# Moving the latent branch's queries, index scores and attention units to later slots in a two-layer encoder kernel

## The reference

```
score = jnp.einsum('bqh,bhqs->bqs', wib, jax.nn.relu(dots))      # C's indexer
_, idx = lax.top_k(score, topk)                                   # 64 of up to 256 keys
...
merged = (gates[:, :, 0] * (ya @ a_w_out) + gates[:, :, 1] * (yb @ b_w_out)
          + gates[:, :, 2] * (yc @ c_w_out) + gates[:, :, 3] * (yd @ d_w_out))
x = x + merged @ w_o
```

## Time and profile before

| | us |
|---|---|
| median of 3 runs | 822.85 (822.40 to 823.03) |
| profiled execution | 822.7 |
| its span, first to last instruction | 821.0 |
| TensorE busy | 804.7 |
| VectorE busy | 560.2 |
| ScalarE busy | 404.1 |
| TensorE's idle before act_lo (L1005) | 6.5 |
| TensorE's idle before x's load | 4.9 |
| TensorE's idle before w_lo (L988) | 1.7 |

### The profile page before, as it was taken

The page is one execution under the profiler, slowest core; times in us unless marked ns, Lnnn a source line. Parts: engine busy times, 40 slices in busy tenths (PEclk is TensorE's granted clock), DMA queues, the critical chain, the costliest instruction groups (busy, mean ns, idle before and its releaser), DMA issues.

```text
span 821.0 us, 10180 instructions
## 1 busy us (share of the span) xinstructions
PE 804.7 (98%) x3860; PEld 657.5 (80%) x3860; DVE 560.2 (68%) x841; ACT 404.1 (49%) x553; POOL 45.1 (5%) x84
## 2 busy tenths in 40 slices
PE   4999999999999999999999999999999999999998
PEld 3888777778888888888888877777788888888886
DVE  8789687894675664456568987798685764565443
ACT  5757455453364444344356656556342644444430
POOL 6240000000000000000004100000000000000000
PEclk8999999999999999999999999999999999999999
DMA  7735446465375655565664545364545564665541
GB/s 204 284 102 182 139 163 211 134 201 202 96 246 175 205 180 179 169 208 190 176 209 136 172 153 180 113 220 157 201 156 192 166 206 155 206 203 185 174 154 51
DMA packets 99681, 144.38 MB, mean 176 GB/s; under 512 B 12081, under 2 KB 63025, under 8 KB 99633
## 3 DMA queue, kind: packets, MB, share of 16 engines
q1 hardware_dynamic: 99632, 143.73, 54.0%
HBM read 142.54 MB, written 1.05 MB: 175 GB/s over the span
## 4 chain that ended last, share of the span: by engine, by line
PE 90%; DVE 5%; SPq 2%; DMA 1%; POOL 1%; issue 1%; ACT 1%; DVEq 0%; ACTq 0%
PE big L1432 18%; PE big L1436 18%; PE big L1435 18%; PE mix L1436 10%; PE mix L1432 10%; PE mix L1435 10%; DVE w_lo L988 2%; SPq L552 1%; PE mix L1765 1%; PE mix L1458 1%; DMA w_raw<-in_w_in 1%; PE mix L1547 1%; POOL rstd L626 1%; PE mix L1502 1%; PE mix L1535 1%
## 5 line engine op out<-in xcount | busy, mean ns | idle before, releaser
L647 ACT ACTIVATE w_hi<-w_raw 128x2048 fp32r<-128x2048 f32 (+2 forms) x140 | 256.6, 1837 | 160.6 <-DMA w_raw<-in_w_gate_up 88.1
L988 DVE TENSOR_TENSOR w_lo<-w_raw,w_hi 128x2048 fp32r<-128x2048 f32 (+3 forms) x139 | 301.1, 2181 | 44.0 <-ACT w_hi L647 43.5
L1432 PE MATMUL big<-w_hi,act_hi 128*128 128x512 f32 (+2 forms) x480 | 188.7, 393 | 8.2 <-DVE act_lo L1005 6.5
L1435 PE MATMUL big<-w_lo,act_hi 128*128 128x512 f32 (+2 forms) x480 | 183.9, 383 | 0.0
L1436 PE MATMUL big<-w_hi,act_lo 128*128 128x512 f32 (+2 forms) x480 | 183.7, 383 | 0.0
L1432 PE MATMUL mix<-w_hi,act_hi 128*128 128x512 f32 x352 | 137.4, 390 | 0.0
L1436 PE MATMUL mix<-w_hi,act_lo 128*128 128x512 f32 x352 | 137.1, 390 | 0.0
L1435 PE MATMUL mix<-w_lo,act_hi 128*128 128x512 f32 x352 | 137.0, 389 | 0.0
L1432 PEld LDWEIGHTS big<-w_hi,act_hi 128*128 128x128 f32 x480 | 90.8, 189 | 30.0 <-DVE act_lo L1005 7.2
L1436 PEld LDWEIGHTS big<-w_hi,act_lo 128*128 128x128 f32 x480 | 90.8, 189 | 17.5
L1435 PEld LDWEIGHTS big<-w_lo,act_hi 128*128 128x128 f32 x480 | 91.0, 190 | 15.5
(11 more groups left out here) (190 smaller groups left out, 696.1 us busy)
## 6 DMA issues: line engine op xcount, KB each, us to landing
w_raw<-in_w_in SPq DMA_DIRECT2D x44, 1024.0 KB, 5.1
w_raw<-in_w_gate_up SPq DMA_DIRECT2D x88, 512.0 KB, 4.8
w_raw<-in_w_down SPq DMA_DIRECT2D x22, 1024.0 KB, 4.9
w_raw<-in_w_o SPq DMA_DIRECT2D x8, 1024.0 KB, 5.1
w_raw<-in_b_w_out SPq DMA_DIRECT2D x4, 1024.0 KB, 5.4
w_raw<-in_w_in SPq DMA_DIRECT2D x4, 904.0 KB, 6.1
w_raw<-in_w_in SPq DMA_DIRECT2D x4, 512.0 KB, 3.6
w_raw<-in_a_w_out SPq DMA_DIRECT2D x4, 512.0 KB, 4.0
```

The lines of the kernel that those rows point to most:

```text
L647: nc.scalar.activation(high(u), arrived(u), ACT.Copy).then_inc(hi_ready.sem, 1)
L988: nc.vector.tensor_tensor(low(u)[:, a:], arrived(u)[:, a:], high(u)[:, a:].bitcast(F32), ALU.subtract).then_inc(lo_by_dve, 1)
L1432: ins = nc.tensor.matmul(dst[:, 0:w], xh, wh, start=first and n == 0, stop=False)
L1435: nc.tensor.matmul(dst[:, 0:w], xh, wl, start=False, stop=False)
```

## The change

- B's keys keep their place in slots 5 and 6 (two heads). C's four queries are normed and rotated in VectorE's steps of slot 12, behind C's key and behind a wait for TQ's second half; they go to `roped_a`, which B's queries used. Their signal is a new one, `J`.
- TK turns two pairs (one bank) in slot 8; the other two pairs become TJ in slot 16.
- TensorE's index products move from slots 7 and 9 to 10 and 14; VectorE's `index_scores` from 7 and 9 to 12 and 15 (`INDEXED_AT`), ScalarE's copies with the products.
- In the bank list the products of block 1 (banks 0 and 1) now stand between S of unit 0 and S of unit 1.
- The attention units 4 and 5 (C's) take all their steps two slots later: S in 23 and 25, T in 25 and 27, Y in 26 and 28.
- The selection rounds are spread anew: slots 12, 15, 16, 17 have 3, 1, 2, 2 rounds of block 0 (before: 12 and 16 with 5 and 3), slots 18, 20, 21, 22, 23 have 2, 2, 1, 2, 1 of block 1 (before: 18, 20, 21, 22 with 1, 3, 2, 2).

```diff
@@ -140,11 +140,13 @@
-PE_AT = {"wT": 3, "latT": 4, "TI": 5, "kv": 6, "idx0": 7, "TK": 8, "idx1": 9, "TQ": 11, "TC": 15,
+PE_AT = {"wT": 3, "latT": 4, "TI": 5, "kv": 6, "TK": 8, "idx0": 10, "TQ": 11, "idx1": 14, "TC": 15, "TJ": 16,
          "spatial": 12, "mixed": 12, "yaT": 13, "ydT": 14}
-S_AT = [13 + 2 * i for i in range(len(ATTN))]
-T_AT = [15 + 2 * i for i in range(len(ATTN))]
-Y_AT = [16 + 2 * i for i in range(len(ATTN))]
+
+S_AT = [13, 15, 17, 19, 23, 25]
+T_AT = [15, 17, 19, 21, 25, 27]
+Y_AT = [16, 18, 20, 22, 26, 28]
+INDEXED_AT = (12, 15)
 def mixer_uses():
@@ -153,15 +155,18 @@
     uses = turned("hT")
     uses += [(("wT",), 0), (("latT",), 1), (("TI", 0), 2), (("TI", 1), 3), (("kv",), 0),
-             (("idx", 0, 0), 0), (("idx", 0, 1), 1), (("TK", 0), 2), (("TK", 1), 3), (("idx", 1, 0), 0), (("idx", 1, 1), 1),
+             (("TK", 0), 2), (("idx", 0, 0), 0), (("idx", 0, 1), 1),
              (("TQ", 0), 2), (("TQ", 1), 3), (("spatial",), 1), (("mixed",), 2),
-             (("yaT",), 3), (("S", 0, 0), 0), (("S", 0, 1), 1), (("ydT", 0), 2), (("ydT", 1), 3), (("TC",), 3)]
+             (("yaT",), 3), (("S", 0, 0), 0), (("S", 0, 1), 1), (("idx", 1, 0), 0), (("idx", 1, 1), 1),
+             (("ydT", 0), 2), (("ydT", 1), 3), (("TC",), 3)]
     for i, (m, _, tb) in enumerate(ATTN):
         if i + 1 < len(ATTN):
             for k in range(2):
                 uses.append((("S", i + 1, k), k))
         for k in range(turned_blocks(i)):
             uses.append((("T", i, k), 2 + k))
+        if i == 0:
+            uses.append((("TJ", 0), 2))
         uses.append((("Y", i), 3 if m == "B" else 2))
     uses += turned("mT") + turned("h2T")
@@ -199,8 +204,9 @@
 DVE_ANGLES = 3 + len(TURNS) + 2 + len(TWO_PI) + 2
 DVE_CONSTS = DVE_ANGLES + 2 + 2 * len(D_POOLS)
-TOPK_AT = {12: (0, 0, 5), 16: (0, 5, 8), 18: (1, 0, 1), 20: (1, 1, 4), 21: (1, 4, 6), 22: (1, 6, 8)}
-DVE_STEPS = 123
+TOPK_AT = {12: (0, 0, 3), 15: (0, 3, 4), 16: (0, 4, 6), 17: (0, 6, 8), 18: (1, 0, 2), 20: (1, 2, 4), 21: (1, 4, 5),
+           22: (1, 5, 7), 23: (1, 7, 8)}
+DVE_STEPS = 132
 class Signal:
@@ -336,7 +342,7 @@
         act_lo_ready = signal_from_1("act_lo_ready", 8)
         lat_normed = signal("lat_normed", 1)
         wt_masked = signal("wt_masked", 1)
-        roped = {n: signal(f"roped_{n}", 1) for n in "IKQC"}
+        roped = {n: signal(f"roped_{n}", 1) for n in "IKQCJ"}
         za_squared = signal("za_squared", 2)
         gelu_arg = signal("gelu_arg", 2)
         gelu_tanh = signal("gelu_tanh", 2)
@@ -806,7 +812,9 @@
                             drain(l, logits[:, odd::2, 0:keys(tb)], "idx", tb, odd,
                                   src=score_view(mix_bank("idx", tb, odd), tb), func=ACT.Relu, scale=SCALE * 0.5)
                 if s == PE_AT["TK"]:
-                    drain_pairs(l, "TK", 7, 2)
+                    drain_pairs(l, "TK", 7, 1)
+                if s == PE_AT["TJ"]:
+                    drain_pairs(l, "TJ", 9, 1)
                 for tb in range(TB):
                     if s == 9 + tb:
                         act.wait_ge(*gelu_arg.nth(l, tb + 1))
@@ -1044,9 +1052,9 @@
             def norm_heads(l, name, tile, tb, gains):
-                heads = tile.shape[2]
-                v = tile[:, tb]
-                step(l, nc.vector.tensor_tensor(v, v, norm_factor(l, name)[:, 0:heads].unsqueeze(2)
+                first, heads = gains[0][0], gains[-1][1] - gains[0][0]
+                v = tile[:, tb, first:first + heads]
+                step(l, nc.vector.tensor_tensor(v, v, norm_factor(l, name)[:, first:first + heads].unsqueeze(2)
                                                 .to_broadcast([P, heads, HD]), ALU.mult))
                 for h0, h1, g in gains:
                     last = nc.vector.tensor_tensor(tile[:, tb, h0:h1], tile[:, tb, h0:h1],
@@ -1267,8 +1275,8 @@
                     if s == 4 + tb:
                         head_squares(l, f"K{tb}", 6)
                     if s == 5 + tb:
-                        norm_heads(l, f"K{tb}", heads_b, tb, [(0, 2, 1), (2, 6, 2)])
-                        rope(l, "K", heads_b, roped_b, tb, 6, [(0, 2, 2, 0), (2, 6, 1, 4)], tb == 1)
+                        norm_heads(l, f"K{tb}", heads_b, tb, [(0, 2, 1)])
+                        rope(l, "K", heads_b, roped_b, tb, 2, [(0, 2, 2, 0)], tb == 1)
                     if s == 6 + tb:
                         head_squares(l, f"Q{tb}", 8)
                     if s == (7, 9)[tb]:
@@ -1285,9 +1293,12 @@
                     step(l, ins)
                     for tb in range(TB):
                         rope(l, "C", heads_c, roped_c, tb, 1, [(0, 1, 2, 0)], tb == 1)
+
+                    dve.wait_ge(*mix_is_full(l, "TQ", 1))
+                    for tb in range(TB):
+                        norm_heads(l, f"K{tb}", heads_b, tb, [(2, 6, 2)])
+                        rope(l, "J", heads_b[:, :, 2:6], roped_a, tb, 4, [(0, 4, 1, 0)], tb == 1)
                 for tb in range(TB):
-                    if s == PE_AT[f"idx{tb}"]:
-                        index_scores(l, tb)
                     if s == 8 + tb:
                         gelu_args(l, tb)
                     if s == 10 + tb - (1 if tb else 0):
@@ -1298,6 +1309,9 @@
                     v_norm(l)
                 if s == PE_AT["spatial"]:
                     gated(l)
+                for tb in range(TB):
+                    if s == INDEXED_AT[tb]:
+                        index_scores(l, tb)
                 if s == PE_AT["yaT"]:
                     y_low(l, 1, y_ac_hi[:], y_ac_lo[:], 0.5, "yaT")
                 if s == PE_AT["ydT"]:
@@ -1580,7 +1594,10 @@
                         scores(l, ("idx", tb), tb, 0, 2)
                 if s == PE_AT["TK"]:
                     pe.wait_ge(*roped["K"].nth(l, 1))
-                    turn_pairs(l, "TK", 7, roped_b, 4)
+                    turn_pairs(l, "TK", 7, roped_b, 2)
+                if s == PE_AT["TJ"]:
+                    pe.wait_ge(*roped["J"].nth(l, 1))
+                    turn_pairs(l, "TJ", 9, roped_a, 2)
                 if s == PE_AT["TQ"]:
                     pe.wait_ge(*roped["Q"].nth(l, 1))
                     turn_pairs(l, "TQ", 3, roped_a, 4)
```

## The result

The changed kernel takes 829.39 us (median of four runs, 828.44 to 830.47) where the kernel before takes 822.94 in the same comparison: ratio 1.008, interval 1.0068 to 1.0091. It is slower, as forecast, but by 6.5 us instead of 2.0, and outside the range. Run again later it took 826.74 us (five runs, 826.59 to 828.29; ratio 1.0052, 1.0038 to 1.0066), which lies inside the range; experiments 10 and 11 take up the difference. The profiled execution took 829.98 us, 828.2 of span. A few executions took over 1000 us (one each of experiments 5 and 7, two of the kernel before); ranges and ratios leave them out, the medians count them (at most 0.2 us lower without), and as the one of experiment 5 is the one that was traced, that experiment is read by its times alone.

What follows compares the result with a forecast made beforehand. TensorE, busy 98% of the span, was taken as the bound, so only its waits could be gained. With a new bank wait at slot 14, 822.7+0.66 (layer 0)+1.45 (layer 1) = 824.8 us, range 821.0 to 827.0.

Steps and rivals of the forecast that it cites:

- The old wait and its price: Slot 10: TensorE's wait for unit 11's low weights goes in both layers, -1.30 and -0.97 us.
- The landing and VectorE's chain: Unit 13 lands at 72.04 us, VectorE enters slot 12 at 79.1, unit 0's row maximum is there at 96.2.
- TensorE's arrival: Layer 0: slot 13's last matmul comes at 95.40 us; TensorE then waits 2.1 us for the S0 banks at slot 14.
- Behind slot 14: Later work stays covered: no second wait at unit 17, unit 23 or T3, costed at nothing.
- the three uncertain margins: Unit 17's split 0.7 us in hand, unit 23's 1.4, T3's row 0.5; if short, up to 1 us each.
- TJ costs its 0.43 us: Slot 16: the other half of the turns, moved there from slot 8, adds 0.43 us.
- The attention units' move: S4/S5 units moved by two slots, taken as free: as many groups, as many slots that hold one.
- Layer 0 to slot 17: Layer 0 is 0.23 us behind at slot 14's ydT, plus 0.43 for TJ in slot 16: +0.66 us.
- the term of the late load: Layer 1, unit 12's load: +1.03 us if on time, +2.85 if as late as before; +1.45 taken.
- halfway: Layer 1: lateness of unit 12's load taken halfway, delaying the chain 0.4 us, for +1.45 us.
- my sum: Whole kernel: 822.7+0.66+1.45 = 824.8 us.
- The clock: Rival: the new slot 14 wait drops TensorE's clock, costing 2 to 3 us a layer, 830 us; chance 3%.

Runs made afterwards that it cites:

- 10: The changed kernel run again unaltered: 826.74 us (five runs), ratio 1.0052 against the kernel before.
- 11: The changed kernel run a third time unaltered, for a second trace of it: 826.77 us for the single look.
- experiment 5: Changed kernel with the latent queries put back in slots 5 and 6, turned in slot 8, no TJ: 820.81 us, ratio 0.9976.
- 7: As experiment 5 (index scores' move alone), with the first three selection rounds in slot 13: 820.48 us, ratio 0.9968.
- experiment 1: Changed kernel with slot 12's three selection rounds moved to slot 13, behind unit 0's row maximum: 820.47 us, ratio 0.9973.
- experiment 4: Kernel before with only the latent queries' norm, rotation and turn moved (slot 12 and TJ): 823.89 us, ratio 1.0013.
- 12: As experiment 4, with VectorE alone combining block 1's index scores in slot 10 rather than 9: 823.32 us, ratio 1.0007.
- experiment 3: Changed kernel with nine unread products on TensorE ahead of block 1's index scores in slot 14: 825.26 us, ratio 1.0035.
- 8: As experiment 3, with four unread products instead of nine: 826.91 us, ratio 1.0045.
- experiment 6: Changed kernel with the ydT mixing products ahead of block 1's index scores on TensorE in slot 14: 826.28 us, ratio 1.0038.
- 9: Changed kernel with one selection round more in slot 12, moved ahead from slot 15: 830.08 us, ratio 1.0089.
- 2: Changed kernel with one of slot 12's three selection rounds put into slot 13: 823.38 us, ratio 1.0007.

## Why the prediction was right in its mechanism and wrong in its size

**The old wait and its price: right.** No wait on w_lo is left, and experiment 1 gains 2.3 us where 1.30+0.97 were counted, although it pays the 0.35 us of the attention units (below) out of it. That the 4.04 us of index scores suffice for it is shown by the times of experiment 5 and the trace of 7; that the queries' part alone does not end it, by experiment 4.

**The landing and VectorE's chain: right.** ScalarE took up unit 13 at 72.00 us (72.04 forecast), VectorE came to slot 12 at 79.14 (79.1) and the row maximum ended at 96.15 (96.2). From VectorE's timeline of the changed kernel:

```profile
79.14 0.47 DVE L1290 SCALAR_TENSOR_TENSOR heads_c<-heads_c,rstd,g_head 128x64 f32<-128x64 f32 x2
...
95.98 0.17 DVE L1159 TENSOR_SCALAR row<-row 128x4 f32<-128x4 f32 x1
```

**TensorE's arrival: right within 0.3 us.** The last matmul of slot 13 started at 95.13 instead of 95.40, so the wait was 2.4 us of pitch (2.69 less the usual 0.32) instead of 2.1.

**Behind slot 14: right.** No wait stands at unit 17, unit 23 or T3; the three uncertain margins held, at nothing. (In experiments 4 and 12 the margin of unit 17 did not hold, for about 0.25 us.) TJ costs its 0.43 us (between slots 15 and 17 the distance to the kernel before grows from 1.74 to 2.17 us).

**The attention units' move: a small term put at nothing.** I took it as free, "as many groups, as many slots that hold one". The count was wrong: from slot 21 on TensorE's small groups stand in six places before (144.85, 151.54, 157.84, 164.96, 171.16 and 177.62 us) and in seven after (146.94, 152.96, 159.25, 171.06, 178.21, 184.36 and 190.80). From slot 17 to behind these groups the distance grows from 2.17 to 2.35 us in layer 0 and from 7.07 to 7.24 in layer 1, about what entering and leaving one more group cost by my own count, 0.2 us. It grows by 0.18 us in layer 0 of experiments 1 and 7 as well, which move these units, and not at all in that of 4 and 12, which don't. No run took the move back alone.

**Layer 0 to slot 17: right but for the clock.** The first matmul of slot 17 in the two layers, of the changed kernel and then of the kernel before:

```profile
121.98 0.48 PE L1446 MATMUL big<-w_hi,act_hi 128*128 128x512 f32 x1
...
527.74 0.48 PE L1446 MATMUL big<-w_hi,act_hi 128*128 128x512 f32 x1
```

```profile
119.81 0.48 PE L1432 MATMUL big<-w_hi,act_hi 128*128 128x512 f32 x1
...
520.67 0.48 PE L1432 MATMUL big<-w_hi,act_hi 128*128 128x512 f32 x1
```

Layer 0 is 2.17 us behind there. Less 1.56 for the clock that is 0.61, where +0.66 was forecast; experiments 3 and 8, whose clock stayed at full, are 0.70 us behind at the same place.

**Layer 1: the term of the late load, too small.** The distance grows from 2.17 to 7.07 us; 0.28 of that comes in before layer 1's slot 6 (454.60 against 452.15 us at its first matmul), 0.18 of it by the attention units' move, and 0.1 has no cause that I found. Of the other 4.62, the clock is 2.59 and 2.03 are left, where I took 1.45, between 1.03 with the load on time and 2.85. The load of unit 12 was late again:

```profile
473.14 1.92 ACT L653 ACTIVATE w_hi<-w_raw 128x2048 fp32r<-128x2048 f32 x1 [2.15 <-DMA w_raw<-in_w_in]
...
476.52 0.69 DVE L1120 SCALAR_TENSOR_TENSOR probs_t<-merged,probs_t 128x512 f32<-128x512 f32 x1 [3.49 <-ACT merged L821]
```

ScalarE stood 1.2 to 2.25 us for it in all ten traces that could be read of a version with the index scores moved, much as in the one of before, so that "halfway" had no ground. The price of the late load varies with it. Counted the same way, layer 1 cost 2.03, 1.80 and 1.65 us in the three traces of the changed kernel, 1.29 in experiment 3 (ScalarE stood 1.23 us) and 3.20 in experiment 8 (2.25 us). The forecast of 1.45 lies among them, its span of 1.03 to 2.85 almost covers them (the 1.03 is itself 0.07 more than its terms, 0.66 and 0.3, give). The cause of the late load was not tried. Without the clock, the profiled execution would have taken 829.98-4.15 = 825.8 us: my sum, this 0.6, and 0.4 of which nearly all is the attention units' move. Experiment 3, in which the clock never falls in slot 14, took 825.26.

**The clock: the step that failed.** The sum took the wait of 2.1 us at its length alone, with nothing for the clock behind it. I wrote that a 1.03 us wait left it at full, one of more than 2 us at the start did not (that one was 6.0 us long by the timeline), and that "waits of 2 to 4 us lie between", and gave the fall 3%. The forecast itself put waits of 2.1 us and more, twice, into that unknown stretch. Nothing in the trace of before spoke for 3%; the price that I gave (2 to 3 us a layer, 830 us) was a little high (1.56 and 2.59 us were measured), and the case should have had a large share of the chances and the upper end of the range. In the three traces it fell in one layer or both, at 1.5 to 4.15 us in all; the mean clocks of the other executions speak for the same. The Trainium skill ("TensorE: Matmul & The Clock Gate", "HAM oscillation"), which I named beside it, says that waits of TensorE drop the clock and each drop is paid again: the traces agree, with 1.56 and 2.59 us in the two layers of one execution. The page speaks of longer gaps than most of these; here the measurement decides.

## What to carry to other kernels

When work is moved off a late engine, follow the engine that becomes early to its next shared buffer and look in which order that buffer is granted: here TensorE came 3 us earlier to banks that are free only behind VectorE's row maximum, and moving three selection rounds behind the row maximum, the change of one number, turned 829.4 us (or 826.7) into 820.5. A new wait of some 2 us on a TensorE that has none is to be priced with a fall of the clock behind it, and filled with other products if it cannot be removed. Moving work off an engine gains only if the next thing in its order isn't pinned to someone else, as the queries' move alone shows.

## What the runs showed of the hardware that I had not expected

How long TensorE stood idle in one wait does not by itself tell whether the granted clock falls. Idle time ahead of block 1's scores in slot 14, and the clock behind it, in the ten traces where that time could be read (experiment 3's has no record of the clock; its matmuls keep their length):

| run | layer 0: idle us, clock | layer 1: idle us, clock |
|---|---|---|
| changed kernel | 2.30, fell | 3.21, fell |
| changed kernel again (10) | 2.48, fell | 2.99, full |
| changed kernel again (11) | 2.12, fell | 2.82, full |
| four rounds (9) | 3.08, full | 3.68, fell |
| four products (8) | 1.39, full | 2.77, full |
| mixing products first (6) | 1.64, full | 1.63, fell |
| half the rounds (2) | 1.22, full | 1.55, full |
| nine products (3) | 0.26, full | 0.44, full |
| rounds in slot 13 (1, 7) | none, full | none, full |

It fell after 1.63 us and stayed at full after 3.08. In the case of 1.63 the ydT products, on 64 rows only, stood ahead of the wait, so that its short time may not be the whole matter; but layer 0 of the same trace had them too, and kept its clock. Among these traces it never fell after less than 1.6 us and, of the nine waits above 2 us, fell after five. The Trainium skill ("TensorE: Matmul & The Clock Gate", "Part 1: The HAM clock gate") says that what the chip measures runs free of the program, and that the same kernel can differ from run to run; the traces agree, with the same code that lost both layers' clock in one execution and only layer 0's in two others, and with falls that come from 1.2 us before the wait's end (layer 1 of the changed kernel) to 1.6 us behind it (layer 1 of experiment 6), 0.6 us after the wide matmuls had begun again. That this is the cause was not shown by an experiment: nothing here sets where in that measure a wait falls. The stretch at half clock also differs: by the windows above, about 3.4 us long in layer 0 and 6.8 in layer 1 (the shares missing from 1.00, times two), for a price of 1.56 and 2.59 us.
